# One lone fp32 product behind the first two slabs of every MLP and feed-forward part

## The chip, the cores and the metric

The kernel runs on one core of one Trainium2 chip. The metric is the device time of one execution in microseconds, from the first to the last instruction with what lies around them. Engines are called as in the profile: PE is TensorE's matrix unit, PEld its weight loads, DVE is VectorE, ACT ScalarE, POOL GpSimd, SP the queue that issues most DMAs.

## The reference, cut to what matters

Two blocks of a language model run one behind the other on 256 tokens of width 1024, in fp32. The first has four layers, each a mixer (gated delta rule, mLSTM, differential attention, gated delta rule) and an MLP. The second has two layers of feed-forward, hybrid mixer, cross attention, feed-forward.

```python
def sq_relu_mlp(h, w1, w2):
    return jnp.square(jax.nn.relu(h @ w1)) @ w2            # w1 1024 x 4096, w2 4096 x 1024

def swiglu(h, w_gate, w_up, w_down):
    return (jax.nn.silu(h @ w_gate) * (h @ w_up)) @ w_down  # 1024 x 2816 twice, 2816 x 1024

# first block, layers 0 to 3
x = x + rms_norm(mixer(rms_norm(x, g0)), g1)
x = x + rms_norm(sq_relu_mlp(rms_norm(x, g2), mlp_w1[i], mlp_w2[i]), g3)
# second block, layers 0 and 1
x = x + 0.5 * swiglu(rms_norm_2(x, ffn1_norm[l]), ...)
x = x + hybrid_mixer(...)
x = x + memory_cross_attention(...)
x = x + 0.5 * swiglu(rms_norm_2(x, ffn2_norm[l]), ...)
```

So there are eight large parts of the same kind: four MLPs and four feed-forwards (ffn1 and ffn2 of two layers).

## The kernel before

All activations stand channel by channel on the 128 partitions, 256 tokens along the free axis, in SBUF for the whole run. Weights come in slabs of 128 x 2048 fp32 (1 MB) through a ring of three buffers, in the order in which they are used. For accuracy at the speed of the fp32r type, each slab is split in two: ScalarE copies it rounded into `wH` (the high half, line 1138), VectorE subtracts that from the slab into `wL` (the low half, line 1618). Both have two buffers. The activation `hT` is split likewise into `hH` and `hL`. A product of weights and activations is the sum of three products of fp32r: high by high, high weight by low activation, low weight by high activation.

In an MLP, slabs 0 to 15 hold `w1`, 256 output channels each: 8 chunks of the contraction x 2 halves of output x 3 products = 48 products of 128 x 128 weights by 256 columns. Slabs 16 to 31 hold `w2`, also 48 products each. A feed-forward has 22 slabs of 48 products for gate and up and 11 of 48 for down. An MLP's part runs as `mlp(i)` (TensorE's part at line 619): `norm_sum` adds up the squares of `x` over the channels with eight true fp32 products of the constant `ones` by the squares, into bank 7; `first_products` (slabs 0 and 1 together, into banks 4 and 5, since the activation's pieces come one by one); `to_channels` for slabs 2 to 15, into bank 4 + j % 4, so slab 2 goes into bank 6; `down_product` into banks 0 to 3; and again `norm_sum`. `ffn(kind, l)` (line 628) has the same shape. In the mixers there are fp32 products between slabs: in the diff mixer `rotate(g)` (line 947), one product of 128 x 128 constants by 512 columns behind a slab; in the gdn mixer the decay and transpose products.

The order of work on each engine is written out by hand, instruction by instruction, and engines wait for each other on semaphores: TensorE waits on `high_split` and `low_split` for a slab's halves, ScalarE on `products_done` before it overwrites a high half, SP on `low_split` before it refills the ring. All matmuls go through the helper `mm`, so most have line 458 in the profile, and operands tell them apart: `ps<-hH,wH` is a product of the high halves, `ps<-sq,ones` one of the norm sums.

Of the kernel before, what the change touches and what calls it, by code (L numbers as in the profile page):

```python
# [15 lines left out]
P = 128  # L16
T = 256
# [124 lines left out]
def program(nc, io, out, parts=None):  # L142
# [23 lines left out]
    with ExitStack() as ctx:  # L166
        def sb(name, shape, dt=F32):
            return ctx.enter_context(nc.sbuf_tensor(name, shape, dt))
# [3 lines left out]
        def sem(name):  # L172

            if not name.startswith(SHARED):
                name = scope[0] + name
            if name not in sems:
                sems[name] = ctx.enter_context(nc.semaphore(name))
            return sems[name]
# [39 lines left out]
        ones = sb("ones", [P, T])  # L218
# [14 lines left out]
        ps = ctx.enter_context(nc.psum_tensor("ps", [P, 8, 512], F32))  # L233
# [219 lines left out]
        def _(pe):  # L453
# [3 lines left out]
            def mm(o, l, r, start, stop, **k):  # L457
                return pe.matmul(o, l, r, start=start, stop=stop, **k)  # L458

            def high(n, c):  # L460
                pe.wait_ge(sem("high_split"), n + 1)
                return wH[:, n % PARTS, :].rearrange("p (c n) -> p c n", c=c)

            def low(n, c):
                return wL[:, n % PARTS, :].rearrange("p (c n) -> p c n", c=c)

            def three(dst, w, x, chunks, before=None, first=True, last=True, second="x"):


                ins = None  # L470
                for pair in (((0, 0), (0, 1), (1, 0)) if second == "x" else ((0, 0), (1, 0), (0, 1))):
                    for k in range(chunks):
                        if before:
                            before(pair, k)
                        ins = mm(dst, w[pair[0]](k), x[pair[1]](k), first and pair == (0, 0) and k == 0,
                                 last and pair == ((1, 0) if second == "x" else (0, 1)) and k == chunks - 1,
                                 **({"skip_group_check": True} if chunks == 1 else {}))
                return ins
# [8 lines left out]
            def bank_of(j):  # L487
                return 4 + j % 4

            def first_products(name, layer, js, c, at):  # L490


                n = [slab_no[(name, layer, j)] for j in js]
                high_w = [high(n[0], c), high(n[1], c)]
                low_w = [low(n[0], c), low(n[1], c)]
                pe.wait_ge(sem("low_split"), n[0] + 1)

                def both_halves(b, w, x, k, ends=False):
                    for m in range(2):
                        ins = mm(ps[:, 4 + b, m * T:(m + 1) * T], at(w, k, m), x[:, k, :],  # L500
                                 w is high_w[b] and x is hH and k == 0 and m == 0, ends and k == DC - 1 and m == 1,
                                 skip_group_check=True)
                    return ins

                for k0 in range(0, DC, 2):
                    pe.wait_ge(sem("hH_ready"), W.next("hH_ready"))
                    for b, w in ((0, high_w[0]), (0, low_w[0]), (1, high_w[1])):
                        for k in (k0, k0 + 1):
                            both_halves(b, w, hH, k)
                for k in range(DC):  # L510
                    if k % 2 == 0:
                        pe.wait_ge(sem("hL_ready"), W.next("hL_ready"))
                    last = both_halves(0, high_w[0], hL, k, ends=True)
                last.then_inc(sem("products_done"), 1)
                for k in range(DC):
                    both_halves(1, high_w[1], hL, k)
                pe.wait_ge(sem("low_split"), n[1] + 1)
                for k in range(DC):
                    last = both_halves(1, low_w[1], hH, k, ends=True)
                last.then_inc(sem("products_done"), 1)  # L520
# [4 lines left out]
            def to_channels(name, layer, j, bank, src=(hH, hL), free=None):  # L525

                n = slab_no[(name, layer, j)]
                wh, wl = high(n, DC), low(n, DC)
                if free and j >= 4:
                    pe.wait_ge(sem(free), W.next(free))  # L530
                for m in range(2):
                    last = three(ps[:, bank, m * T:(m + 1) * T],
                                 [lambda k: wh[:, k, m * P:(m + 1) * P], lambda k: wl[:, k, m * P:(m + 1) * P]],
                                 [lambda k: src[0][:, k, :], lambda k: src[1][:, k, :]], DC,
                                 low_weights(n, (1, 0)) if m == 0 else None)
                last.then_inc(sem("products_done"), 1)

            def to_tokens(name, layer, j, bank, src=(hH, hL)):
# [7 lines left out]
                                 low_weights(n, (0, 1)) if i == 0 else None, second="w")  # L546
                last.then_inc(sem("products_done"), 1)

            def norm_sum(bank=7):

                for c in range(4):
                    pe.wait_ge(sem("sq_ready"), W.next("sq_ready"))
                    for k in (2 * c, 2 * c + 1):
                        last = mm(ps[:, bank, 0:T], ones[:, 0:P], sq[:, k, :], k == 0, k == DC - 1)
                last.then_inc(sem("ss_ready"), 1)
# [42 lines left out]
            def down_product(name, layer, chunks, waited):  # L598

                for j in range(chunks // 2):  # L600
                    n = slab_no[(name, layer, j)]
                    wh, wl = high(n, 2), low(n, 2)
                    for kk in (2 * j, 2 * j + 1):
                        if kk in waited:
                            pe.wait_ge(sem("hidden_ready"), W.next("hidden_ready"))
                        end = kk == chunks - 1
                        for m in range(DC):
                            last = three(ps[:, m // 2, (m % 2) * T:(m % 2 + 1) * T],
                                         [lambda k: wh[:, kk % 2, m * P:(m + 1) * P],
                                          lambda k: wl[:, kk % 2, m * P:(m + 1) * P]],  # L610
                                         [lambda k: hidH[:, kk, :], lambda k: hidL[:, kk, :]], 1,
                                         low_weights(n, (1, 0)) if m == 0 and kk % 2 == 0 else None,
                                         first=kk == 0 and m % 2 == 0, last=end and m % 2 == 1)
                            if end and m % 2:
                                last.then_inc(sem("products_done"), 1)
                    if not end:
                        last.then_inc(sem("products_done"), 1)

            def mlp(i):
                norm_sum()  # L620
                first_products("mlp_w1", i, (0, 1), DC, columns)
                for j in range(2, 16):
                    to_channels("mlp_w1", i, j, bank_of(j), free="bank_read")
                down_product("mlp_w2", i, 32, range(0, 32, 2))
                pe.wait_ge(sem("bank_read"), W.next("bank_read", 4))
                norm_sum()

            def ffn(kind, l):
                norm_sum()
                first_products(kind, l, (0, 1), 2 * DC, lambda w, k, half: w[:, half * DC + k, :])  # L630
                for n in range(2, 22):
                    u = slab_no[(kind, l, n)]
                    wh, wl = high(u, 2 * DC), low(u, 2 * DC)
                    if n >= 4:
                        pe.wait_ge(sem("bank_read"), W.next("bank_read"))
                    for half in range(2):
                        last = three(ps[:, 4 + n % 4, half * T:(half + 1) * T],
                                     [lambda k: wh[:, half * DC + k, :], lambda k: wl[:, half * DC + k, :]],
                                     [lambda k: hH[:, k, :], lambda k: hL[:, k, :]], DC,
                                     low_weights(u, (1, 0)) if half == 0 else None)  # L640
                    last.then_inc(sem("products_done"), 1)
                down_product(f"{kind}_w_down_2", l, 22, range(22))
                pe.wait_ge(sem("bank_read"), W.next("bank_read", 4))
# [1499 lines left out]
```

## Time and profile before

| | us |
|---|---|
| median of three runs | 2967.17 |
| lowest, highest | 2961.21, 2976.12 |
| the profiled execution | 2963.2 |
| its span, first to last instruction | 2961.5 |
| TensorE matmuls busy | 2782.7 |
| VectorE busy, ScalarE busy | 1636.2, 1354.9 |

The profile describes one execution. Busy times overlap between engines, and matmuls are pipelined: a record's duration is longer than the distance to the next record's start, so the pace of a stream is read from the number of records in a stretch, not from their durations. The chain that ended last is followed back from the last instruction, at each step to what released it.

### The profile page before, as it was taken

Reading aid. Unit: us, or ns where it says so; the run is one execution under the profiler, and the core shown is the slowest. Engines: PE = TensorE matmul, PEld = TensorE weight load, DVE = VectorE, ACT = ScalarE, POOL = GpSimd, SP = SyncE. Lnnn points to the kernel's source line nnn. Section 1 sums busy time; section 2 is a strip of 40 time slices with the busy share of each in tenths; the row PEclk is TensorE's granted clock in tenths of the full one; section 3 lists DMA queues with packets and bytes.
Section 4 is the critical chain, followed back from the end, with each engine's and each line's share of the span. In section 5 each row is a group of like instructions: output and inputs, shape, how many; then the busy total and the mean of one; then the engine's idle time right before and its main releaser. Section 6 shows DMA issues by size and latency. Waiting matters only on the chain.

```text
span 2961.5 us, 50099 instructions
## 1 busy us (share of the span) xinstructions
PE 2782.7 (94%) x22378; PEld 2686.7 (91%) x22378; DVE 1636.2 (55%) x1941; ACT 1354.9 (46%) x1597; POOL 75.7 (3%) x92
## 2 busy tenths in 40 slices
PE   7998999999998999998999999899999999799998
PEld 7888998889887998888998998889999998789998
DVE  6665644455466645765645545654555545754553
ACT  4624534454445534544544435444544435444443
POOL 1200000000000000200000000000000000000000
PEclk9999999999999999999999999999999999899999
DMA  6402654345451554511555654334665755324663
GB/s 191 151 15 70 199 189 130 111 153 190 154 164 52 185 186 128 157 43 43 185 189 150 187 186 143 100 101 141 178 194 171 195 191 155 100 86 143 171 185 114
DMA packets 426631, 427.94 MB, mean 145 GB/s; under 512 B 8274, under 2 KB 397760, under 8 KB 426288
## 3 DMA queue, kind: packets, MB, share of 16 engines
q1 hardware_dynamic: 426064, 424.37, 46.1%
q8 instruction: 177, 2.90, 0.4%
q0 software_dynamic: 352, 0.36, 0.0%
q14 instruction: 38, 0.31, 0.0%
HBM read 423.65 MB, written 1.05 MB: 143 GB/s over the span
## 4 chain that ended last, share of the span: by engine, by line
PE 89%; ACT 5%; DVE 4%; issue 1%; DMA 0%; SPq 0%; POOL 0%; ACTq 0%; DVEq 0%; POOLq 0%
PE ps L458 88%; ACT wH L1138 1%; PE ps L768 1%; DVE wL L1618 1%; DVE hT L1629 1%; DMA const<-shape_constants 0%; ACT rs L1155 0%; DVE sq L1657 0%; ACT rs L1156 0%; ACT hH L1172 0%; DVE xT L1660 0%; ACT sq L1161 0%; PE ps L906 0%; ACT arena L1304 0%; ACT L1151 0%
## 5 line engine op out<-in xcount | busy, mean ns | idle before, releaser
L1618 DVE TENSOR_TENSOR wL<-ring,wH 128x2048 fp32r<-128x2048 f32 x400 | 916.5, 2291 | 962.0 <-ACT wH L1138 961.7
L1138 ACT ACTIVATE wH<-ring 128x2048 fp32r<-128x2048 f32 x400 | 767.8, 1920 | 1206.7 <-PE ps L458 1190.8
L458 PE MATMUL ps<-hH,wH 128*128 128x256 f32 x4160 | 592.8, 285 | 44.0 <-ACT hH L1172 42.9
L458 PE MATMUL ps<-hidden_parts,wH 128*128 128x256 f32 x3712 | 627.8, 278 | 1.2 <-ACT wH L1138 1.2
L458 PEld LDWEIGHTS ps<-hH,wH 128*128 128x128 f32 x4160 | 535.3, 193 | 59.3 <-issue 58.9
L458 PE MATMUL ps<-hH,wL 128*128 128x256 f32 x4160 | 573.3, 280 | 1.6 <-DVE wL L1618 1.6
L458 PEld LDWEIGHTS ps<-hidden_parts,wH 128*128 128x128 f32 x3712 | 553.4, 188 | 1.4 <-DVE hidden_parts L2052 1.4
L458 PE MATMUL ps<-hL,wH 128*128 128x256 f32 x4160 | 552.4, 278 | 0.0
L458 PEld LDWEIGHTS ps<-hH,wL 128*128 128x128 f32 x4160 | 524.5, 190 | 1.9 <-DVE wL L1618 1.8
L458 PEld LDWEIGHTS ps<-hL,wH 128*128 128x128 f32 x4160 | 512.4, 189 | 0.0
L458 PE MATMUL ps<-hidden_parts,wL 128*128 128x256 f32 x1856 | 497.2, 278 | 0.1
L458 PEld LDWEIGHTS ps<-hidden_parts,wL 128*128 128x128 f32 x1856 | 341.9, 189 | 0.3 <-DVE wL L1618 0.3
L458 PE MATMUL ps<-arena 128*128 128x128 f32 (+1 forms) x1776 | 285.6, 310 | 56.5 <-DVE arena L1994 30.4
L458 PEld LDWEIGHTS ps<-arena 128*128 128x128 f32 x1776 | 249.3, 200 | 77.0 <-issue 22.5
L458 PE MATMUL ps<-sq,ones 128*128 128x256 f32 (+1 forms) x488 | 151.8, 462 | 46.3 <-ACT sq L1161 29.8
L458 PEld LDWEIGHTS ps<-sq,ones 128*128 128x128 f32 x488 | 99.9, 215 | 79.1 <-ACT sq L1161 33.4
L1629 DVE SCALAR_TENSOR_TENSOR hT<-xT,vec,rs 128x256 f32<-128x256 f32 x136 | 55.4, 480 | 54.1 <-ACT rs L1156 54.1
L1328 ACT ACTIVATE arena<-ps 128x512 f32<-128x512 f32 x48 | 28.7, 597 | 94.3 <-PE ps L768 94.3
L1161 ACT ACTIVATE sq<-xT 128x512 f32<-128x512 f32 x68 | 41.8, 630 | 43.9 <-DVE xT L1660 24.1
L1765 DVE SCALAR_TENSOR_TENSOR arena<-arena 128x256 f32<-128x256 f32 x144 | 60.4, 484 | 0.0
L1657 DVE SCALAR_TENSOR_TENSOR sq<-ps,vec,rs 128x256 f32<-128x256 f32 x64 | 27.9, 477 | 44.9 <-ACT rs L1156 44.9
L458 PE MATMUL ps<-arena,const 128*128 128x256 f32 (+2 forms) x176 | 49.5, 369 | 2.0 <-ACT arena L1377 1.1
(247 smaller groups left out, 1842.2 us busy)
## 6 DMA issues: line engine op xcount, KB each, us to landing
ring<-in_mlp_w SPq DMA_DIRECT2D x128, 1024.0 KB, 5.2
ring<-in_ffn_w_gate SPq DMA_DIRECT2D x88, 512.0 KB, 4.0
ring<-in_ffn_w_up SPq DMA_DIRECT2D x88, 512.0 KB, 5.3
ring<-in_ffn_w_down SPq DMA_DIRECT2D x44, 1024.0 KB, 4.9
ring<-in_gdn_w_in SPq DMA_DIRECT2D x32, 1024.0 KB, 5.7
ring<-in_w_in SPq DMA_DIRECT2D x28, 1024.0 KB, 5.4
ring<-in_mlstm_w_in SPq DMA_DIRECT2D x12, 1024.0 KB, 5.3
ring<-in_diff_w_in SPq DMA_DIRECT2D x12, 1024.0 KB, 5.1
```

Of the source, the lines that this page charges most:

```text
L458: return pe.matmul(o, l, r, start=start, stop=stop, **k)
L768: last = pe.transpose(ps[:, 2 + q % 2, h * P:(h + 1) * P], inv[:, t, h0 + h, :], ident)
L1138: f(wH[:, n % PARTS, :], ring[:, n % RING, :], ACT.Copy).then_inc(sem("high_split"), 1)
L1161: f(sq[:, 2 * c:2 * c + 2, :], src(c), ACT.Square).then_inc(sem("sq_ready"), 1)
L1328: f(invT[:, q // 2, 4 * (q % 2):4 * (q % 2) + 4, :], ps[:, 2 + q % 2, :].rearrange("p (h n) -> p h n", h=4), ACT.Copy)\
L1618: tt(wL[:, n % PARTS, :], ring[:, n % RING, :], wH[:, n % PARTS, :].bitcast(F32), ALU.subtract)\
L1629: stt(hT[:, c, :], xT[:, c, :], column(gain, k0 + c), rs[:, :], ALU.mult, ALU.mult)\
L1657: ins = stt(sq[:, k, :], ps[:, c, (k % 2) * T:(k % 2 + 1) * T], column("norm_g", k0 + k), rs[:, :], ALU.mult, ALU.mult)
L1765: ins = stt(dst, src, w, dst, ALU.mult, ALU.add)
```

## The change

TensorE's stream gets a function `lone_product`: one true fp32 product of the constant `ones` (128 x 128 as weights, 256 columns as the moving operand) into the first half of bank 6 of PSUM. It waits for nothing and signals nothing, and nobody reads what it leaves: the next slab's products begin with `start` in the same bank and overwrite it. It is called once in each MLP and each feed-forward, directly behind `first_products`.

```diff
+            def lone_product():
+
+                mm(ps[:, 6, 0:T], ones[:, 0:P], ones[:, 0:T], True, True)
+
             def norm_sum(bank=7):
...
             def mlp(i):
                 norm_sum()
                 first_products("mlp_w1", i, (0, 1), DC, columns)
+                lone_product()
                 for j in range(2, 16):
...
             def ffn(kind, l):
                 norm_sum()
                 first_products(kind, l, (0, 1), 2 * DC, lambda w, k, half: w[:, half * DC + k, :])
+                lone_product()
                 for n in range(2, 22):
```

In the built order TensorE has eight rows more; the other engines have the same rows as before. At the first place, in MLP 0, TensorE's order before reads as follows: the last products of slabs 0 and 1 together, then slab 2.

```order
L458 MATMUL ps<-hL,wH 128x256 [waits hL_ready]
L458 MATMUL ps<-hL,wH 128x256 x19
L458 MATMUL ps<-hH,wL 128x256 [waits low_split]
L458 MATMUL ps<-hH,wL 128x256 x15
L458 MATMUL ps<-hH,wH 128x256 [waits high_split]
L458 MATMUL ps<-hH,wH 128x256 x7
L458 MATMUL ps<-hL,wH 128x256 x8
L458 MATMUL ps<-hH,wL 128x256 [waits low_split]
```

And the same place of the changed kernel:

```order
L458 MATMUL ps<-hL,wH 128x256 [waits hL_ready]
L458 MATMUL ps<-hL,wH 128x256 x19
L458 MATMUL ps<-hH,wL 128x256 [waits low_split]
L458 MATMUL ps<-hH,wL 128x256 x15
L458 MATMUL ps<-ones 128x256
L458 MATMUL ps<-hH,wH 128x256 [waits high_split]
L458 MATMUL ps<-hH,wH 128x256 x7
L458 MATMUL ps<-hL,wH 128x256 x8
```

The lone product, `ps<-ones`, stands between the first two slabs' last product and slab 2's wait for its high half. Nothing else moved. The feed-forwards' four places read the same. For comparison, TensorE's order before in the diff mixer around one of its rotations, which the change leaves alone:

```order
L458 MATMUL ps<-hL,wH 128x256 x8
L458 MATMUL ps<-hH,wL 128x256 x8
L458 MATMUL ps<-arena,const 128x512 [waits dif_roped,dif_raw_ready]
L458 MATMUL ps<-hH,wH 128x256 [waits high_split]
L458 MATMUL ps<-hH,wH 128x256 x7
L458 MATMUL ps<-hL,wH 128x256 x8
```

Here an fp32 product of 512 columns stands between two slabs already.

## Rows read from the trace of the kernel before

**Rows 1.** The page: engine totals, granted clock in 40 slices, chain that ended last.

```profile
PE 2782.7 (94%) x22378; PEld 2686.7 (91%) x22378; DVE 1636.2 (55%) x1941; ACT 1354.9 (46%) x1597; POOL 75.7 (3%) x92
...
PEclk9999999999999999999999999999999999899999
...
PE 89%; ACT 5%; DVE 4%; issue 1%; DMA 0%; SPq 0%; POOL 0%; ACTq 0%; DVEq 0%; POOLq 0%
PE ps L458 88%; ACT wH L1138 1%; PE ps L768 1%; DVE wL L1618 1%; DVE hT L1629 1%; DMA const<-shape_constants 0%; ACT rs L1155 0%; DVE sq L1657 0%; ACT rs L1156 0%; ACT hH L1172 0%; DVE xT L1660 0%; ACT sq L1161 0%; PE ps L906 0%; ACT arena L1304 0%; ACT L1151 0%
```

**Rows 2.** The chain in order of time, MLP 0 and MLP 2: start, duration, what.

```profile
278.71 179.14 PE ps L458 x1552
...
958.39 184.61 PE ps L458 x1552
```

**Rows 3.** Windows inside the eight parts: us, busy (records) by engine, PEclk, DMA.

```profile
292.00:452.00 160.00, 160.00 (x1414) 160.00 (x1414) 86.69 (x62) 72.65 (x61) 0.00 (x0) 1.00 0.60 197
627.00:786.00 159.00, 159.00 (x1405) 159.00 (x1405) 85.73 (x61) 72.08 (x61) 0.00 (x0) 1.00 0.61 198
970.00:1136.00 166.00, 166.00 (x1412) 166.00 (x1411) 86.34 (x63) 73.13 (x61) 0.00 (x0) 1.00 0.58 188
1420.00:1578.00 158.00, 158.00 (x1396) 158.00 (x1395) 85.43 (x61) 70.81 (x59) 0.00 (x0) 1.00 0.61 198
1610.00:1780.00 170.00, 170.00 (x1446) 170.00 (x1445) 83.18 (x73) 70.36 (x74) 0.00 (x0) 1.00 0.64 188
2100.00:2262.00 162.00, 162.00 (x1432) 162.00 (x1431) 82.01 (x74) 70.00 (x72) 0.00 (x0) 1.00 0.66 197
2290.00:2450.00 160.00, 160.00 (x1414) 160.00 (x1413) 80.61 (x71) 69.95 (x72) 0.00 (x0) 1.00 0.65 196
2780.00:2940.00 160.00, 160.00 (x1361) 160.00 (x1360) 77.31 (x68) 65.04 (x67) 0.00 (x0) 1.00 0.57 172
```

**Rows 4.** PE records by tile, same windows, MLP 0 and 2: ns min/median/max.

```profile
L458 PE MATMUL ps<-hL,wH x224: 276/276/276, 291.9 to 366.2; 128*128 128x256 f32 x112
...
L458 PE MATMUL ps<-hL,wH x224: 281/281/281, 970.7 to 1047.9; 128*128 128x256 f32 x112
```

**Rows 5.** Timeline of PE in the diff mixer: start, us, line, operands, count.

```profile
830.22 1.07 PE L458 MATMUL ps<-hH,wL 128*128 128x256 f32 x8
831.13 1.02 PE L458 MATMUL ps<-arena,const 128*128 128x512 f32 x2
831.58 1.51 PE L458 MATMUL ps<-hH,wH 128*128 128x256 f32 x8
832.92 1.10 PE L458 MATMUL ps<-hL,wH 128*128 128x256 f32 x8
...
837.64 1.02 PE L458 MATMUL ps<-arena,const 128*128 128x512 f32 x2
...
840.38 1.10 PE L458 MATMUL ps<-hH,wL 128*128 128x256 f32 x8
...
850.66 1.02 PE L458 MATMUL ps<-arena,const 128*128 128x512 f32 x2
...
852.44 1.07 PE L458 MATMUL ps<-hL,wH 128*128 128x256 f32 x8
```

**Rows 6.** Timeline of PE, sums of 256 columns in the hybrid and cross mixers.

```profile
1981.85 3.61 PE L458 MATMUL ps<-sq,ones 128*128 128x256 f32 x16
1985.11 1.29 PE L458 MATMUL ps<-hH,wH 128*128 128x256 f32 x8
...
2725.79 3.62 PE L458 MATMUL ps<-arena 128*128 128x256 f32 x16
...
2730.17 1.07 PE L458 MATMUL ps<-hH,wH 128*128 128x256 f32 x8
```

**Rows 7.** Timeline in MLP 0: slab 2's halves on ACT and DVE, its start on PE.

```profile
287.67 1.92 ACT L1138 ACTIVATE wH<-ring 128x2048 fp32r<-128x2048 f32 x1 [6.73 <-PE ps L458]
...
289.63 2.29 DVE L1618 TENSOR_TENSOR wL<-ring,wH 128x2048 fp32r<-128x2048 f32 x1 [4.74 <-ACT wH L1138]
...
291.02 1.07 PE L458 MATMUL ps<-hH,wH 128*128 128x256 f32 x8
```

**Rows 8.** Timeline of PE in the first gdn mixer, behind one group of fp32 products.

```profile
64.61 0.59 PE L458 MATMUL ps<-arena,const 128*128 128x256 f32 x2
...
66.42 1.10 PE L458 MATMUL ps<-hL,wH 128*128 128x256 f32 x8
```

## The prediction, made before the changed kernel ran

> **What bounds the kernel now.** I read the page first: engine totals, slices and granted clock, and the shares of the chain that ended last [rows 1]. TensorE's matmuls are busy for 2782.7 of 2961.5 us and TensorE holds 89% of the chain, 88% at line 458, the helper through which nearly every product goes. So what is put into TensorE's stream in a place where it does not wait lengthens the kernel by its own duration, and what changes the pace of that stream is paid for, or earned, in full.
>
> Then I read the chain in order of time in two MLPs [rows 2]. From its first slab product to the last product of the norm sum behind it, each MLP is one unbroken piece of 1552 TensorE records. The same piece takes 179.14 us in MLP 0 and 184.61 us in MLP 2. Nothing in the program differs between them. The reader should see here that 5.5 us are decided by something other than the program.
>
> The busy time by stretch, cut inside the eight large parts (four MLPs, four feed-forwards), shows what [rows 3]. TensorE is busy for the whole of every window and the granted clock is 1.00 (2.4 GHz) in all eight, so neither waits nor clock make the difference. The number of records does: 160.00 us over 1414 records is 113.2 ns a product in MLP 0; 166.00 over 1412 is 117.6 ns in MLP 2. Every window lies at one of these two paces. Fast: MLP 0, 1, 3 and the windows at 2100 and 2290 (second feed-forward of layer 0, first of layer 1). Slow: MLP 2, the window at 1610 (first feed-forward of layer 0) and the one at 2780 (last feed-forward). The durations of single records say the same: 276 ns from minimum to maximum in MLP 0, 281 in MLP 2 [rows 4]. So a stream of fp32r products runs at a **fast pace** (113.2 ns, record 276) or a **slow pace** (117.6 ns, record 281), 4.4 ns apart, and keeps it for some 1500 products, until something breaks the stream. Three of eight parts happen to be slow in the profiled execution.
>
> **The change, part by part.** It adds one fp32 product of 256 columns in eight places, removes nothing and adds no wait. There are two terms.
>
> First, its **own duration**. An fp32 product leaves two records in the trace (x2 for one, x16 for eight [rows 5, 6]). The nearest row is the diff mixer's rotation, one fp32 product of 512 columns directly between two slabs [rows 5]. It starts at 831.13 and the next slab's first product at 831.58, 0.45 us; that slab's first eight products then last 1.51 us where eight in the stream last 1.10, 0.41 more. That is 0.86 us for 512 columns, 0.43 for 256. The sum over squares in the hybrid mixer gives the same from products of the lone product's own size [rows 6]: eight of them from 1981.85 to 1985.11, 3.26 us, plus 1.29 - 1.10 = 0.19 us for the first eight behind, 3.45 / 8 = 0.43 us. Eight lone products: **+3.5 us**. Does anything hide it? In the stretch behind, TensorE never waits [rows 3], so there is no gap to fall into. It could at most be hidden if slab 2 were late. It isn't: ScalarE's high half of slab 2 is done at 287.67 + 1.92 = 289.59, VectorE's low half at 289.63 + 2.29 = 291.92 [rows 7], and TensorE takes up the first at 291.02 and the second sixteen products of 113 ns later, at 292.8. Both are early by 0.9 to 1.4 us, so a stream that arrives 0.43 us later finds them ready too; nothing turns into a wait. The bounds of this term are 0 and 8 x 0.86 = 7 us.
>
> Second, the **pace behind it**. A fp32 product breaks the fp32r stream, and the stream behind can come out at the other pace. Behind a lone product stand 16 x 48 - 96 + 768 = 1440 products in an MLP and 22 x 48 - 96 + 528 = 1488 in a feed-forward. One part that flips is worth 1440 x 4.4 = 6.3 us or 1488 x 4.4 = 6.5 us. This term therefore runs from -4.4 x (1440 + 2 x 1488) = **-19.4 us** (the three slow ones become fast) to +4.4 x (3 x 1440 + 2 x 1488) = **+32.1 us** (the five fast ones become slow). It is far larger than the first, so the forecast hangs on which pace follows.
>
> The rows that are nearest are again the diff mixer's, since the order is the lone product's: a slab's last hH, wL products, one fp32 product, the next slab's hH, wH products, no wait [rows 5]. Before 831.13 eight products take 1.07 us (fast), after it 1.10 (slow): fast turns slow. At 837.64, the next such product, slow stays slow (1.10 behind it). At 850.66 slow turns fast (1.07 behind). The gdn mixer's fp32 products between slabs turn a stream slow as well [rows 8]: 1.10 us for eight behind those at 64.61. The hybrid's eight sums of 256 columns at 1981.85 turn fast to slow too; the cross mixer's output sums at 2725.79 leave the stream fast [rows 6]. Wherever the same products follow each other without a wait, the outcome tends to repeat. That matters for the odds: the eight places are alike, so I expect the five fast parts to react all in one way, not each by a draw of its own. I take the nearest row: a fast stream comes out slow, a slow one stays slow. **Forecast:** 3.5 + 32.1 = +35.6 us on the profiled execution's 2963.2, 2998.8 us. The median of the runs shown is 2967.17, 4.0 above that execution, and the runs spread from 2961.21 to 2976.12, about two parts' pace; if all eight places come out alike, this part of the spread is gone, so I keep 2999 and don't add the 4.0.
>
> **The rivals.** *All eight come out fast.* For it: the slow stream that turned fast at 850.66, the cross mixer's sums, and that five parts of eight found the fast pace by themselves. Against it: the direct precedent at 831.13. It gives 2963.2 + 3.5 - 19.4 = 2947.3, faster. It decides as soon as more than one slow part gains and no fast one is lost: one flip, 6.4, already outweighs the 3.5 for all eight.
>
> *The pace is left as it is.* Each stream takes up its old pace behind the product, or the pace is set by something that the product doesn't touch. For it: 837.64, slow before and behind. Then only the first term is left, 2966.7, no change. [...]
>
> *Mixed.* Fast turns slow and slow turns fast: 2963.2 + 3.5 + 32.1 - 19.4 = 2979.4. Or each place draws for itself: four of eight slow, one more than now, 2963.2 + 3.5 + 6.4 = 2973.1. Either is within 0.5% of 2967.17.
>
> That the product would not be there at all, merged or dropped, is excluded: the built order shows it in all eight places.
>
> **How the numbers follow.** All slow 0.44; mixed 0.18; pace untouched 0.20; all fast 0.18. Only beyond about 0.5% (15 us) can a measurement of this kernel be told from no change: all slow lies 1.1% above the median, all fast 0.7% below, the other two inside. So faster 0.18, same 0.38, slower 0.44. The range leaves out the fast case alone: from 2960 (pace untouched, 7 us for draws elsewhere) to 3006 (all slow, the first term at 7 us and 4 for the mixers' own draws). The forecast's own range is 2993 to 3006.
>
> **What would show it.** In the profile after: eight pairs of ones-by-ones records, 3.45 / 16 = 0.216 us apart, no idle behind them; the same eight windows shifted, with records of 281 ns in all of them and about 117.6 ns a product; granted clock 1.00 as now. In MLP 0 the piece of the chain grows from 179.14 to about 179.1 + 0.4 + 6.3 = 185.8 us. If its records read 276 behind the lone product, the pace step is wrong. If they read 276 in MLP 2, the fast case holds. If some read one and some the other, the claim that alike places react alike is wrong. If a wait on the high half appears behind the product, the cover of slab 2 was misread.

## The result, and the profile after

| | before, us | changed, us | ratio, 95% interval |
|---|---|---|---|
| first comparison (4 runs each) | 2964.19 (2949.68 to 2976.12) | 3001.57 (2996.76 to 3008.99) | 1.0127 (1.0101 to 1.0153) |
| repeated beside the experiments (21 and 10 runs) | 2972.85 (2954.49 to 2989.72) | 2997.56 (2988.30 to 3008.12) | 1.0080 (1.0051 to 1.0109) |
| profiled execution | 2963.2 | 3005.87 | |

The changed kernel is slower, by 37 us in the first comparison, of which its eight products account for 3.5 us. The profile after, in the views of the rows ahead of the prediction. First the page, then the groups by line and form (line, engine, operands, shapes, count | busy us, mean ns | idle before):

```profile
PE 2824.9 (94%) x22394; PEld 2727.2 (91%) x22394; DVE 1635.3 (54%) x1941; ACT 1354.4 (45%) x1597; POOL 76.5 (3%) x92
...
PEclk9999999999999999999999999999999999899999
```

```profile
L458 PE MATMUL ps<-hidden_parts,wH 128*128 128x256 f32 x3712 | 643.2, 281 | 1.2 <-ACT wH L1144 1.2
```

Against [rows 1], TensorE is busy for 42 us more with 16 records more; VectorE and ScalarE do what they did; the granted clock reads the same. The last row is that of the high weights in the eight down products (3456 of its 3712 records; the other 256 lie in the second block's mixers): its records last 281 ns in the mean, the slow pace's number. Before, the same row had 278.

The chain in order of time, the four MLPs and the feed-forwards (start, us, what), against [rows 2]:

```profile
280.25 186.03 PE ps L458 x1554
621.61 186.03 PE ps L458 x1554
973.37 187.53 PE ps L458 x1554
1424.21 184.64 PE ps L458 x1554
1621.35 188.39 PE ps L458 x1586
2113.53 186.83 PE ps L458 x1586
2306.82 188.43 PE ps L458 x1586
2800.46 190.29 PE ps L458 x1602
```

Each MLP's piece has two records more, the lone product's. MLP 0 went from 179.14 to 186.03 us. MLP 2, slow before already, went from 184.61 only to 187.53.

The eight windows, one in each part, all behind the lone product (us, busy and records of PE, PEld, DVE, ACT, POOL, granted clock, DMA), against [rows 3]:

```profile
295.00:455.00 160.00, 160.00 (x1361) 160.00 (x1360) 84.16 (x60) 69.15 (x59) 0.00 (x0) 1.00 0.58 191
636.00:795.00 159.00, 159.00 (x1352) 159.00 (x1352) 82.94 (x60) 69.52 (x60) 0.00 (x0) 1.00 0.57 190
990.00:1150.00 160.00, 160.00 (x1361) 160.00 (x1360) 84.15 (x60) 68.77 (x58) 0.00 (x0) 1.00 0.58 191
1438.00:1596.00 158.00, 158.00 (x1344) 158.00 (x1343) 82.28 (x59) 68.65 (x58) 0.00 (x0) 1.00 0.58 190
1637.00:1795.00 158.00, 158.00 (x1344) 158.00 (x1343) 77.90 (x72) 65.63 (x69) 0.00 (x0) 1.00 0.65 190
2127.00:2285.00 158.00, 158.00 (x1344) 158.00 (x1343) 78.33 (x71) 65.51 (x70) 0.00 (x0) 1.00 0.64 190
2322.00:2480.00 158.00, 158.00 (x1344) 158.00 (x1343) 78.23 (x71) 65.50 (x70) 0.00 (x0) 1.00 0.64 189
2814.00:2972.00 158.00, 158.00 (x1344) 158.00 (x1343) 78.27 (x71) 65.51 (x70) 0.00 (x0) 1.00 0.62 187
```

The reader should divide: 160.00 / 1361 and 158.00 / 1344 are both 117.6 ns. All eight are slow, still with no wait and at a clock of 1.00. The timeline of TensorE at the first place shows the moment:

```profile
290.81 1.98 PE L458 MATMUL ps<-hH,wL 128*128 128x256 f32 x16
292.63 0.59 PE L458 MATMUL ps<-ones 128*128 128x256 f32 x2
292.87 1.29 PE L458 MATMUL ps<-hH,wH 128*128 128x256 f32 x8
294.00 1.10 PE L458 MATMUL ps<-hL,wH 128*128 128x256 f32 x8
```

Sixteen products in 1.98 us, the fast pace (the slow one takes 2.05); two records of the lone product, no idle at either end; then, past the eight that overlap it, eight in 1.10, the slow pace. In the trace the four distances between starts around the lone product are 115, 215, 27 and 305 ns, 662 in all. The same four steps were read at all eight places, within 1 ns, and all eight streams were fast ahead of it and slow behind.

### The profile page after: what moved, and what is told of

It is laid out like the page before. It is cut to its first block, busy times and chain, and to the rows that moved or that the text cites. A ratio compares the mean times of both kernels' runs of the same rounds, so it can differ in the third digit from the quotient of the medians.

```text
span 3004.1 us, 50131 instructions
## 1 busy us (share of the span) xinstructions
PE 2824.9 (94%) x22394; PEld 2727.2 (91%) x22394; DVE 1635.3 (54%) x1941; ACT 1354.4 (45%) x1597; POOL 76.5 (3%) x92
## 4 chain that ended last, share of the span: by engine, by line
PE 90%; ACT 5%; DVE 4%; issue 1%; DMA 0%; SPq 0%; POOL 0%; ACTq 0%; DVEq 0%; POOLq 0%
PE ps L458 88%; ACT wH L1144 1%; PE ps L774 1%; DVE hT L1635 1%; DVE wL L1624 1%; DVE sq L1663 0%; ACT rs L1161 0%; DVE xT L1666 0%; ACT rs L1162 0%; ACT hH L1178 0%; DMA ring<-in_gdn_w_in 0%; ACT sq L1167 0%; PE ps L912 0%; ACT L1157 0%; ACT arena L1310 0%
## 5 line engine op out<-in xcount | busy, mean ns | idle before, releaser
L458 PE MATMUL ps<-hH,wH 128*128 128x256 f32 x4160 | 603.1, 288 | 44.0 <-ACT hH L1178 42.9
L458 PE MATMUL ps<-hidden_parts,wH 128*128 128x256 f32 x3712 | 643.2, 281 | 1.2 <-ACT wH L1144 1.2
L458 PEld LDWEIGHTS ps<-hH,wH 128*128 128x128 f32 x4160 | 543.6, 195 | 60.3 <-issue 59.4
L458 PE MATMUL ps<-hH,wL 128*128 128x256 f32 x4160 | 580.3, 282 | 1.8 <-DVE wL L1624 1.8
L458 PEld LDWEIGHTS ps<-hidden_parts,wH 128*128 128x128 f32 x3712 | 561.0, 190 | 1.4 <-DVE hidden_parts L2058 1.4
L458 PE MATMUL ps<-hL,wH 128*128 128x256 f32 x4160 | 558.7, 280 | 0.0
L458 PEld LDWEIGHTS ps<-hH,wL 128*128 128x128 f32 x4160 | 530.6, 191 | 2.2 <-DVE wL L1624 2.2
L458 PEld LDWEIGHTS ps<-hL,wH 128*128 128x128 f32 x4160 | 518.8, 189 | 0.0
```

## The experiments

The question was what in the product chooses the pace: its length (an alignment within the stream), its type (fp32 among fp32r), or nothing (a draw each time, the outcome changing from one execution to the next). The experiments read one quantity: the pace of a stream ahead of and behind an inserted product. "Fast" and "slow" are the two paces, 113.3 and 117.8 ns from one product's start to the next.

### An fp32 product of another width ahead of each slab

```diff
+            WIDTHS = (256, 512, 128, 384, 64, 192, 320, 96, 448, 32, 160, 224, 288, 16)
             def lone_product():
-                mm(ps[:, 6, 0:T], ones[:, 0:P], ones[:, 0:T], True, True)
+                n = WIDTHS[probes[0] % 14]
+                probes[0] += 1
+                mm(ps[:, 0, 0:n], ones[:, 0:P], cc("tree_ts")[:, 0:n], True, True)
...
-                lone_product()
                 for j in range(2, 16):
+                    lone_product()
                     to_channels("mlp_w1", i, j, bank_of(j), free="bank_read")
```

Each part begins the row of widths at another place (cut here).

> The lone product of the change is replaced by one fp32 product ahead of every slab from 2 on in all eight parts (136 in all), of 14 widths in turn (256, 512, 128, 384, 64, 192, 320, 96, 448, 32, 160, 224, 288, 16 columns), into bank 0, with a mask from the constants as moving operand; each MLP and feed-forward begins the row of widths at another place. Theory A (alignment): the pace behind a product depends on how many cycles it takes, so the same width behind the same pace gives the same pace again in nearly every place, and some widths give the fast pace, some the slow. At 256 columns behind a fast stream: slow, always. Theory B (type switch): every fp32 product in an fp32r stream leaves the slow pace, whatever its width; then all 136 stretches behind are slow. Theory C (a draw each time): the same width gives now one pace, now the other, 256 too. Time under A with half of the stretches slow: the before kernel's 2964 plus 136 products with a mean of 205 columns, 0.35 us each, 47 us, plus 5 us of pace: about 3015. Under B: 3043.

3031.3 us, beside 2972.0 for the kernel before, one run each, and 16 us over what I had expected. By the distances between starts the products added 56.5 us and not 47, since each of the five widths from 16 to 128 costs 0.22 us, and 95 of the 136 stretches behind were slow, not half. Each inserted product is a trial, though not an independent one: a width always follows the same other width, so it mostly meets the stream in the same state. Counted over the trace, by the pace ahead:

| columns | behind a fast stream | behind a slow stream |
|---|---|---|
| 16 | none | 9 stay slow |
| 32 | 1 stays fast | 9 turn fast |
| 64 | 2 stay fast | 6 turn fast, 2 stay slow |
| 96 | 2 stay fast | 6 stay slow, 2 turn fast |
| 128 | none | 7 turn fast, 2 stay slow |
| 160, 192 | 18 turn slow | 2 stay slow |
| 224, 288 | none | 19 stay slow |
| 256 | 1 turns slow | 8 turn fast, 1 stays slow |
| 320 | none | 8 stay slow, 2 turn fast |
| 384 | 6 turn slow | 2 stay slow, 2 turn fast |
| 448, 512 | 11 turn slow | 8 stay slow |

TensorE's timeline at two of them, in MLP 0:

```profile
344.87 0.30 PE L458 MATMUL ps<-const,ones 128*128 128x32 f32 x2
345.01 1.17 PE L458 MATMUL ps<-hH,wH 128*128 128x256 f32 x8
346.02 1.07 PE L458 MATMUL ps<-hL,wH 128*128 128x256 f32 x8
...
350.56 0.43 PE L458 MATMUL ps<-const,ones 128*128 128x160 f32 x2
350.72 1.21 PE L458 MATMUL ps<-hH,wH 128*128 128x256 f32 x8
351.77 1.10 PE L458 MATMUL ps<-hL,wH 128*128 128x256 f32 x8
```

Thirty-two columns are followed by the fast pace, 160 by the slow one. Behind a fast stream the width decided in every one of 41 trials: up to 96 columns the stream stayed fast (5 of 5), at the six widths from 160 on that met a fast stream it turned slow (36 of 36). Behind a slow stream one more thing counts: its distances are 117, 118 or 119 ns, and the inserted product starts 120 or 118 to 119 ns behind the last one. At 256 columns the eight that started at 118 to 119 turned fast, the one at 120 stayed slow; at 320 and 384 the four at 118 turned fast and the ten at 120 stayed slow. At 16 columns the nine at 118 to 119 stayed slow, so the start alone has no fixed meaning. 64 and 128 columns gave both outcomes at 120 ns (6 to 2 and 7 to 1).

The weight loads of the same trace part those too. In the slow stream the record of every third load lasts 192 ns and those of the two others 187 or 188, so the inserted product can stand at one of three positions: the long load is that of the stream's last product (A), of the inserted product's first record (B) or of its second (C; these are the starts at 118 to 119). At 64 columns all six at B turned fast and both at A stayed slow; at 128 the seven at B turned fast, and the one at A and the one at C stayed slow. Sorted by width, pace ahead and position, no group among the 136 holds two outcomes. A draw each time is refuted, and so is the rival that every fp32 product is followed by the slow pace. Neither the bank nor the data seem to matter to the one width that both kernels have: 256 columns behind a fast stream, here in a single trial into bank 0 with a mask as operand, show the same four distances as the lone product, 662 ns in all.

### The same with fp32r products

```diff
+            def lone_product(w):
...
+                mm(ps[:, 0, 0:n], w, hH[:, 0:2, :].rearrange("p c t -> p (c t)")[:, 0:n], True, True)
...
                 for m in range(2):
+                    if m and free == "bank_read":
+                        lone_product(wh[:, 0, 0:P])
... (the same between the halves of each slab in `ffn`)
```

> As the run with 136 fp32 products, but the additional product is of type fp32r (the slab's high weights by hH, the same 14 widths in turn, into bank 0) and stands between the two halves of each slab's products, since its weights are the slab's. Theory A (alignment): a product of an irregular number of columns breaks the stream too, so some widths change the pace; only those whose length keeps the alignment (256 above all, which is the stream's own width) never do. Theory B (type switch): no fp32r product changes the pace, each part keeps from its third product on the pace with which it began, 276 or 281 ns in all its records. Time: 136 products of 205 columns in the mean at 0.09 us each add 12 us, so about 2976 plus or minus 15 for the pace.

2988.9 us, beside the same 2972.0. Products of the stream's own type move the pace as well. From 16 to 96 columns all 28 behind a fast stream turned it slow; 160 and 192 left all 20 slow streams slow; 320 and 448 swapped both ways without exception (16 slow to fast, 4 fast to slow); **384 was followed by the fast pace ten times of ten**, seven behind a fast and three behind a slow stream. The ten of 256 columns, the stream's own width, changed nothing, as expected. 224 and 512 gave both outcomes behind slow streams, and again the position of the long weight load parts them without exception. One of the swaps, by 128 columns at 711.00, shows in TensorE's timeline, where the additional product is merged with the eight of its slab:

```profile
710.06 1.11 PE L458 MATMUL ps<-hH,wL 128*128 128x256 f32 x8
711.00 1.21 PE L458 MATMUL ps<-hH,wH 128*128 128x128 f32 x9
712.05 1.07 PE L458 MATMUL ps<-hL,wH 128*128 128x256 f32 x8
```

The type switch is out: it's neither needed nor sufficient. What is left is how long the disturbance lasts and where in the stream's pattern it falls; why a given length does what it does is not shown.

### The lone product in the MLPs alone

```diff
             def ffn(kind, l):
...
-                lone_product()
                 for n in range(2, 22):
```

> The lone product in the four MLPs alone. Theory (the pace behind the product is fixed by it): all four MLPs read 281 ns behind the product, whatever their pace ahead of it, and the feed-forwards read as they would without the change, some 276 and some 281. Against the before kernel of the same chip, whose MLPs are slow in one of four or so: 3 x 6.3 + 4 x 0.43 = about +20 us, give or take the draws at the parts' beginnings (6.4 each). Rival (a draw at each product): one or two of the four MLPs stay fast, +8 us or so.

2995.4 us, 23 more than the kernel before beside it. Its windows, the last two MLPs and the first two feed-forwards:

```profile
990.00:1140.00 150.00, 150.00 (x1276) 150.00 (x1275) 80.56 (x58) 65.73 (x58) 0.00 (x0) 1.00 0.57 190
1440.00:1590.00 150.00, 150.00 (x1276) 150.00 (x1275) 78.29 (x58) 65.69 (x56) 0.00 (x0) 1.00 0.57 187
1640.00:1790.00 150.00, 150.00 (x1326) 150.00 (x1326) 77.52 (x69) 65.07 (x69) 0.00 (x0) 1.00 0.66 196
2130.00:2280.00 150.00, 150.00 (x1276) 150.00 (x1275) 73.48 (x66) 63.13 (x66) 0.00 (x0) 1.00 0.64 189
```

In 150 us 1276 records are the slow pace and 1326 the fast one. All four MLPs are slow behind the product, each fast ahead of it, so that a slow stream stays slow was not tried here; of the untouched feed-forwards two are fast and two slow, as in the kernel before. The effect stays where the product is. A single time of this run proves little, since the parts' own draws are as large; the windows do.

### Two lone products in place of one

```diff
             def lone_product():
                 mm(ps[:, 6, 0:T], ones[:, 0:P], ones[:, 0:T], True, True)
+                mm(ps[:, 6, 0:T], ones[:, 0:P], ones[:, 0:T], True, True)
```

> Two lone products of 256 columns, one behind the other, in each of the eight places. Theory A (alignment): the second product adds 0.43 us per place, 3.5 us in all, and moves the stream by one more product's length; all eight places again come out alike, but not necessarily slow: if fast, the time is about 2964 - 3 x 6.4 + 6.9 = 2952, if slow 3001.6 + 3.5 = 3005. Theory B (type switch): all slow, 3005, for certain. Theory C (draws): mixed.

2953.6 us beside 2972.0, one run each: twice the added work in less time. Seven parts were fast behind the pair (six of them ahead of it as well, one slow ahead), one slow ahead stayed slow, so that not all eight came out alike, as I had expected of them. That all would be slow is refuted. The same kernel again, with ten runs:

> Two lone products of 256 fp32 columns in each place, timed. In its one profile seven of eight parts were fast behind them. Theory A: again most or all fast; a slow part at most where the stream ahead was slow (it has three positions within its pattern of 118, 118, 117 ns, and the outcome may hang on which). Time 2950 to 2957, 0.3 to 0.5% under before, about 5 us over the kernel with 32 columns, since two products cost 0.87 us a place and one of 32 columns 0.23.

2959.1 us, 2 over the range that I had expected, ratio 0.9956 (0.9928 to 0.9983). In this profile all four streams that were fast ahead stayed fast; of four slow ones two turned fast and two stayed slow. The two that stayed slow began the pair 118 and 119 ns behind the last product, the two that turned fast at 120. In the first profile both slow streams met the pair at 120 ns, and one turned fast and one stayed slow. The position of the long weight load tells all six apart: the three at B turned fast, the one at A and the two at C stayed slow. A single product of 256 columns does the opposite at B and C. The 2976.6 us of this profiled execution is near the upper end of its runs, with two parts slow.

### One number changed: 32 columns in place of 256

```diff
-                mm(ps[:, 6, 0:T], ones[:, 0:P], ones[:, 0:T], True, True)
+                mm(ps[:, 6, 0:32], ones[:, 0:P], ones[:, 0:32], True, True)
```

> The changed kernel with one number different: the lone fp32 product has 32 columns in place of 256, in the same eight places. Theory A (alignment): in the run with 14 widths a product of 32 fp32 columns left the fast pace ten times of ten (nine of them behind a slow stream, one behind a fast one), so all eight parts read 276 ns behind it. It costs 0.23 us a place there (459 ns from product to product over it against two paces of 113), 1.8 us in all. Time: 2964 + 1.8 - 6.4 x (three to four slow parts) = 2943 to 2950, faster than before by 0.5 to 0.7%, and 50 to 55 us under the change itself. Theory B (any fp32 product leaves the slow pace): 3000, as the change. Theory D (a short product does nothing): 2966.

2954.3 us (2946.97 to 2956.6), ratio 0.9928 (0.9889 to 0.9967) to the kernel before and 43 us under the change beside it. The same product at the same place, of another length, does the opposite:

```profile
292.18 1.98 PE L458 MATMUL ps<-hH,wL 128*128 128x256 f32 x16
294.00 0.30 PE L458 MATMUL ps<-ones 128*128 128x32 f32 x2
294.13 1.17 PE L458 MATMUL ps<-hH,wH 128*128 128x256 f32 x8
295.14 1.07 PE L458 MATMUL ps<-hL,wH 128*128 128x256 f32 x8
```

Five streams were fast ahead and three slow; all eight are fast behind it. The time came out 4 to 11 us over what I had expected, since I had reckoned from the 2964 of the first comparison and the kernel before took 2972.85 here; against that it gained 18.6, where three to four parts less the products' own time would be 17 to 24.

### No fp32 product: 384 columns of fp32r

```diff
+            def lone_product(w):
+
+                mm(ps[:, 0, 0:384], w, hH[:, 0:2, :].rearrange("p c t -> p (c t)")[:, 0:384], True, True)
...
                 for m in range(2):
+                    if m and j == 2 and free == "bank_read":
+                        lone_product(wh[:, 0, 0:P])
... (the same between the halves of slab 2 in `ffn`)
```

> No fp32 product at all: in the eight places one fp32r product of 384 columns (slab 2's high weights by hH, into bank 0), between the halves of slab 2. In the run with fp32r widths this width left the fast pace ten times of ten, seven behind a fast and three behind a slow stream, at 0.17 us a place. Theory A: all eight parts fast behind it, time 2964 + 1.4 - 6.4 x (three to four) = 2943 to 2950. Theory B (the type switch decides): the parts keep the pace with which they began, some slow, 2965 give or take 8.

2949.8 us (2941.14 to 2958.2), ratio 0.9920 (0.9875 to 0.9964), within the expected range. Seven of the eight streams were slow ahead of it, one fast, and all eight were fast behind. MLP 1 in TensorE's timeline, with the product merged into the slab's second eight:

```profile
627.61 1.11 PE L458 MATMUL ps<-hH,wL 128*128 128x256 f32 x8
628.55 1.24 PE L458 MATMUL ps<-hH,wH 128*128 128x384 f32 x9
629.63 1.07 PE L458 MATMUL ps<-hL,wH 128*128 128x256 f32 x8
```

And the group over the eight down products, first in this kernel, then with the 32 columns:

```profile
L458 PE MATMUL ps<-hidden_parts,wH 128*128 128x256 f32 x3712 | 620.2, 276 | 1.2 <-ACT wH L1146 1.2
```

```profile
L458 PE MATMUL ps<-hidden_parts,wH 128*128 128x256 f32 x3712 | 620.1, 276 | 1.2 <-ACT wH L1144 1.2
```

The mean of this one row sorts the kernels: 281 ns in the changed one, 276 in both of these. These two are faster than the kernel before and the changed one, and can't be told apart from each other.

### The change itself again

> The changed kernel itself beside the others on the same chip, with 256 fp32 columns: all eight parts slow behind the product once more, about 3000, 1.2% over the before kernel. If its parts come out otherwise than in its first profile (one of them fast), the claim that the outcome is fixed by the product's length falls.

2997.6 us, 24.7 over the kernel before beside it. The expectation that all eight come out slow failed in one part, and with it the claim that the product's length alone fixes the outcome. Six streams were fast ahead and turned slow, with the same four distances as in the first profile. Two were slow ahead. The last feed-forward's lone product began 120 ns behind the last one and its stream stayed slow. MLP 1's began 118 behind, and the stream turned fast:

```profile
632.95 2.05 PE L458 MATMUL ps<-hH,wL 128*128 128x256 f32 x16
634.83 0.60 PE L458 MATMUL ps<-ones 128*128 128x256 f32 x2
635.08 1.27 PE L458 MATMUL ps<-hH,wH 128*128 128x256 f32 x8
```

The window behind it has the fast pace's 1326 records in 150 us:

```profile
640.00:790.00 150.00, 150.00 (x1326) 150.00 (x1326) 80.11 (x58) 68.49 (x57) 0.00 (x0) 1.00 0.58 195
```

That agrees with the run of widths, where 256 columns at 118 to 119 (position C) turned fast eight times of eight and the one at 120 (position B) stayed slow. So the outcome follows from the product's length, the pace ahead and the place in the slow stream's pattern at which the product begins.

## Why the prediction was right, and where not

**The two paces** as the largest term: right, and the whole result hangs on it. Inside the windows no wait and no lower clock appears, before or after.

**The product's own duration**, 0.43 us a place from the diff mixer's rotation: measured 662 - 2 x 113.3 = 435 ns from distances, 3.5 us in all. That slab 2 would be ready: right, there is no idle behind any lone product.

**A fast stream turns slow**, taken from one row, the rotation at 831.13: right at all eight places of the first profile, four of the MLP-only kernel and six of the repeat, 18 of 18, and in the run of widths once more. That alike places react alike held for fast streams, which fits with a fast stream having no pattern within it: each distance is 113 or 114 and each weight load 187 or 188 ns, so the same product always meets the same state. The rotation has 512 columns and the lone product 256; both turned a fast stream slow, as did every width from 160 on that met one, which the single row could not have shown. With 32 columns the same argument would have given the wrong sign.

The choice of the row was in part luck. The same mixer, in the same trace, held two rotations that leave a fast stream fast, and the prediction weighed neither:

```profile
821.13 1.07 PE L458 MATMUL ps<-hH,wL 128*128 128x256 f32 x8
822.04 1.88 PE L458 MATMUL ps<-arena,const 128*128 128x512 f32 x4
...
824.68 1.07 PE L458 MATMUL ps<-hL,wH 128*128 128x256 f32 x8
...
856.06 1.07 PE L458 MATMUL ps<-hH,wL 128*128 128x256 f32 x8
856.97 1.02 PE L458 MATMUL ps<-arena,const 128*128 128x512 f32 x2
...
858.74 1.07 PE L458 MATMUL ps<-wH,hL 128*128 128x256 f32 x8
```

At 822.04 two rotations follow each other, and two products of 256 columns in a row leave a fast stream fast as well. At 856.97 a single one is followed by products in which weights and activations have changed places, so it matters too what stands behind. Over the ten traces a single rotation behind a fast stream, with the same kind of products on both sides, turned it slow 15 times of 15; with this exchange behind it, it left it fast 5 times of 5. The cross mixer's sums at 2725.79, which the prediction read as leaving a stream fast, have fp32 products ahead of them and say nothing on that.

**A slow stream stays slow**: half right. It was not tested in the first profile, where all eight streams happened to be fast ahead; that no slow one met the product at position C, as MLP 1 did in the repeat, was luck, worth 6.4 us for each such part. The repeat showed both outcomes, told apart by a start at 120 or 118 ns. The rows knew it: 837.64 stayed slow, 850.66 turned fast [rows 5], and I took the first as the nearest without asking what told them apart. In the trace the first starts at 120 ns and position B, the second at 119 and C.

**The sum.** The change's profiled execution took 42.7 us more than the one before, where I had 35.6. By the chain's pieces the eight parts grew by 36.3 us: MLP 0, 1, 2 and 3 by 6.9, 6.8, 2.9 and 5.3; the first and last feed-forward by 0.2 and 0.0 (slow already); the two between by 7.0 and 7.1, once their missing 48 products of 113.3 ns are added to the pieces before (they end at x1536). MLP 2 and 3 stray from 0.4 and 6.8 since part of a piece's beginning runs at half clock in one and not in the other, and MLP 2's first 96 products were slow before and fast now. The other 6.4 us lie outside the parts. Records of 281 ns count 6247 before and 13873 after. Inside the eight parts they grew by 7022 (the 7296 of the prediction less the first products of three parts, slow before and fast now), so 604 more products outside them were slow too, 2.7 us. The granted clock stood at half for 156 us after against 146 before, and 6.7 of those 10 us lie outside the parts; half of them, some 3 us, is an estimate of their cost. Neither belongs to the change, as far as the trace shows.

**That part of the spread would be gone** if all places came out alike: wrong in the main. The changed kernel's ten runs still reach from 2988 to 3008. The first products of each part, the mixers and the parts' half-clock beginnings still differ from execution to execution, and a slow stream ahead can still turn fast.

**The rivals.** "All fast" was not what this product does, though it is just what the same product of 32 columns does. "The pace is left as it is" is refuted by the eight places, and a draw at each place by the 18 of 18. "Mixed" names what the single product does at position C, but the streams behind were slow in 19 of the 20 parts where it stood.

## What to carry to other kernels

In a long unbroken stream of equal matmuls, divide a window's time by its records: if the same code shows two values (here 113.2 and 117.6 ns, record durations of 276 and 281) with no wait and a full clock, 4% lies in how the stream was entered, and no busy share will say so. A short product of the right length in front of the stream can fix it, here 0.17 to 0.23 us for 6.4. Its length has to be found by trial: one run with many widths at many places gave the candidates here, and one run of each confirmed it. It has to be read behind both paces and at all three positions. Nor does it carry over from another place by its length alone: a second product, or other products behind, turned the outcome round. And a kernel with such draws can't be judged by a few times: the kernel before ranges over 35 us, so compare the paces part by part in the traces.

## What the runs showed of the hardware that I had not expected

The pace of fp32r products of 128 x 128 weights by 256 columns has two stable values and goes over within some five products behind a disturbance (one row of distances into the fast one: 119, 121, 116, 114, 114, 113 ns). It then holds for up to 1583 products, across slabs, banks and operands. One fp32r product of 384 columns between those of 256 was followed by the fast pace from either side, 18 times of 18 in two kernels, though it never met a slow stream at one of the three positions; 32 fp32 columns were so 18 times of 18 as well, at all three. The weight loads show the two patterns, here the same products' loads in MLP 0 (fast) and MLP 2 (slow) of the kernel before, ns min/median/max:

```profile
L458 PEld LDWEIGHTS ps<-hL,wH x223: 187/188/188, 291.8 to 365.9; 128*128 128x128 f32 x112
L458 PEld LDWEIGHTS ps<-hL,wH x215: 187/188/192, 970.8 to 1046.9; 128*128 128x128 f32 x108
```

In the slow one every third load is the long one. Its position relative to the inserted product, together with the product's type and width, parts every outcome behind the inserted products, with no exception in any run. This sorting was read from traces already there and was not put to a run of its own. What in the engine keeps the two patterns apart is open: no run here changes the weight loads apart from the products.
